# Reordering the heads and projections of a hybrid attention block on one Trainium2 core

## Time and profile before

| | |
|---|---|
| three runs | 743.0, 746.4, 747.96 us, median 746.4 |
| profiled execution, span from first to last instruction | 740.7 us |
| mean granted TensorE clock in it | 0.969 of full |
| PE busy | 695.3 us, 94% |
| DVE, ACT, POOL busy | 339.0, 278.3, 248.4 us |
| instructions | 9658 |

### The profile page before, as it was taken

How to read it: one execution, slowest core, us unless ns; L and a number is a source line. 1 busy time by engine, 2 the same in 40 slices (tenths; PEclk the granted TensorE clock), 3 DMA queues, 4 the chain that set the end, 5 groups by cost and what they waited for, 6 DMA issues and landing times.

```text
span 740.7 us, 9658 instructions
## 1 busy us (share of the span) xinstructions
PE 695.3 (94%) x3541; PEld 581.9 (79%) x3541; DVE 339.0 (46%) x819; ACT 278.3 (38%) x546; POOL 248.4 (34%) x121
## 2 busy tenths in 40 slices
PE   5998989999897997997999999999999999999995
PEld 4885678997797996786878888888888888888884
DVE  6521377577667778774436334334334321003004
ACT  4401565565454545552454323223223222114112
POOL 6601521031211211023317443544544434434422
PEclk7999999999999998999999999999999999999998
DMA  7447532031121111012315333323233233233202
GB/s 235 82 143 234 163 93 65 8 93 36 36 65 36 39 57 35 2 58 66 87 47 163 93 87 112 87 87 112 86 90 109 86 95 104 86 104 96 86 1 114
DMA packets 84227, 64.42 MB, mean 87 GB/s; under 512 B 2424, under 2 KB 75204, under 8 KB 84180
## 3 DMA queue, kind: packets, MB, share of 16 engines
q1 hardware_dynamic: 80160, 58.83, 26.9%
q10 hardware_dynamic: 3444, 4.48, 1.9%
q0 software_dynamic: 576, 0.49, 0.6%
HBM read 61.67 MB, written 4.47 MB: 89 GB/s over the span
## 4 chain that ended last, share of the span: by engine, by line
PE 84%; DVE 7%; DMA 4%; issue 3%; ACT 2%; SPq 0%; POOL 0%; DVEq 0%; ACTq 0%
PE bank L462 14%; PE bank L464 14%; PE bank L463 14%; PE bank L444 9%; PE bank L445 9%; PE bank L446 9%; PE bank L608 5%; DMA raw<-in_w_in_dram 4%; PE bank L585 3%; PE bank L569 2%; PE bank L570 2%; PE bank L456 2%; PE bank L519 1%; DVE bank L1054 1%; DVE k_diff L1035 1%
## 5 line engine op out<-in xcount | busy, mean ns | idle before, releaser
L420 POOL TENSOR_TENSOR w_lo<-raw,w_hi 128x1024 fp32r<-128x1024 f32 (+1 forms) x96 | 233.7, 2438 | 468.8 <-ACT w_hi L748 468.8
L748 ACT CAST w_hi<-raw 128x1024 fp32r<-128x1024 f32 (+1 forms) x96 | 100.4, 1050 | 275.3 <-PE bank L464 143.9
L462 PE MATMUL bank<-xT_hi,w_hi 128*128 128x512 f32 x480 | 191.9, 400 | 1.8 <-POOL w_lo L420 1.5
L464 PE MATMUL bank<-xT_hi,w_lo 128*128 128x512 f32 x480 | 190.0, 396 | 0.0
L463 PE MATMUL bank<-xT_lo,w_hi 128*128 128x512 f32 x480 | 189.6, 395 | 0.0
L462 PEld LDWEIGHTS bank<-xT_hi,w_hi 128*128 128x128 f32 x480 | 90.9, 189 | 21.7 <-POOL w_lo L420 2.0
L464 PEld LDWEIGHTS bank<-xT_hi,w_lo 128*128 128x128 f32 x480 | 91.0, 189 | 20.6
L463 PEld LDWEIGHTS bank<-xT_lo,w_hi 128*128 128x128 f32 x480 | 91.0, 190 | 18.2 <-issue 0.2
L816 ACT ACTIVATE E<-bank,nmax 128x128 f32<-128x128 f32 (+3 forms) x96 | 50.8, 529 | 76.3 <-DVE nmax L1054 76.2
L446 PE MATMUL bank<-w_hi,act_lo 128*128 128x512 f32 x176 | 69.0, 392 | 0.0
L444 PE MATMUL bank<-w_hi,act_hi 128*128 128x512 f32 x176 | 69.0, 392 | 0.0
(11 more groups left out here) (175 smaller groups left out, 934.2 us busy)
## 6 DMA issues: line engine op xcount, KB each, us to landing
raw<-in_w_gate_dram SPq DMA_DIRECT2D x22, 512.0 KB, 3.9
raw<-in_w_up_dram SPq DMA_DIRECT2D x22, 512.0 KB, 3.9
raw<-in_w_down_dram SPq DMA_DIRECT2D x22, 512.0 KB, 3.8
raw<-in_w_in_dram SPq DMA_DIRECT2D x20, 512.0 KB, 3.9
raw<-in_w_out_dram SPq DMA_DIRECT2D x8, 512.0 KB, 3.8
bias_rows<-bias_scratch ACTq DMA_DIRECT2D x1, 2304.0 KB
xres<-in_x_dram SPq DMA_DIRECT2D x4, 512.0 KB, 5.3
raw<-in_cmp_w_k_dram SPq DMA_DIRECT2D x4, 512.0 KB, 4.4
```

The source lines that it names most:

```text
L420: nc.gpsimd.tensor_tensor(wv_lo(k)[:, 0:n], raw[:, raw_of[("chunk", k)] % RAW_SLOTS, 0:n], wv_hi(k)[:, 0:n].bitcast(F32), ALU.subtract).th ...
L462: nc.tensor.matmul(bank[:, :], hi, xT_hi[:, kt, :], start=kt == 0, stop=False)
L464: return nc.tensor.matmul(bank[:, :], lo, xT_hi[:, kt, :], start=False, stop=kt == KT - 1)
L748: nc.scalar.copy(wv_hi(k)[:, 0:n], raw[:, raw_of[("chunk", k)] % RAW_SLOTS, 0:n]).then_inc(s_whi, 1)
```

## The change

- Order: `PROJ_JOBS` and `OUT_JOBS` name a fixed order of jobs. Compressed keys ("c") and their MLP ("h", "ht", "hc") move from the prologue into the loop, with w1 in four buffers of its own, which share memory with x; x is loaded a second time behind them. Slots: diff(1) comes ahead of nsa(2) and nsa(3).
- Filler: a planner gives each step its pieces by cost and by due steps, in place of a fixed rate. Evacuations are cut in units, which are laid on successive steps on ACT and DVE.
- Keys: for the differential heads the two maps keep their own halves and the second copy is made by four DMAs on POOL's queue (`double_keys`); for the NSA keys ACT writes hi twice and DVE subtracts twice.
- Bias rows are spread for each head by a DMA of SP, between weight loads.
- Roots: 1/sqrt is exp(-0.5 ln(.)), two activations on ACT, in place of Sqrt on ACT and small steps on DVE. In the head ACT takes all four squares. The last norm is made for each of the four tiles.
- w_out: the NSA part ("og") and the differential part ("od") are 4-piece jobs in the two projection banks. The transposes of `mix` are jobs ("mt").
- The last two chunks of w_down are done tile by tile (`last_rows`).
- Matmuls ahead of the head: 12 in place of 16, and 5, 3 and 5 between the row tiles.

```diff
-WARM = 16
+WARM = 12
+WARM_GAP = (5, 3, 5)
 RAW_SLOTS = 3
 SPLIT_SLOTS = 4
+W1_SLOTS = 4
 E_SLOTS = 4
 BIAS_SLOTS = 3
-PIECES = 8
-PIECES_PER_SLOT = 1.35
-LEAD_PIECES = 6
-FILL_RATE = 2.5
+LEAD_JOBS = 1
+AHEAD = {"q": 4, "k": 4, "dq": 4, "dk": 6, "dv": -2, "hc": 3}
...
+PROJ_JOBS = [("q", 0), ("k", "ksl"), ("vg", 0), ("vg", 1), ("k", "kw"),
+             ("q", 1), ("dq", 0), ("dk", 0), ("dv", (0, 0)), ("dv", (0, 1)), ("dq", 1), ("dk", 1), ("q", 2), ("c", 0),
+             ("c", 1), ("q", 3), ("h", 0), ("h", 1), ("dv", (1, 0)), ("ht", 0), ("dv", (1, 1)), ("hc", 0), ("dq", 2), ("dk", 2),
+             ("dk", 3), ("dq", 3)]
+OUT_JOBS = [("mt", 4), ("mt", 5), ("mt", 6), ("mt", 7), ("og", (0, 0)), ("og", (0, 1)), ("og", (0, 2)), ("og", (0, 3)), ("og", (1, 0)),
+            ("mt", 0), ("og", (1, 1)), ("mt", 1), ("og", (1, 2)), ("mt", 2), ("og", (1, 3)), ("mt", 3)]
+OUT_JOBS += [("od", (dh, t)) for dh in range(2) for t in range(NT)]
+BASE_JOBS = 4
+PIECES = {"ht": 1, "hc": 1, "mt": 1, "og": 4, "od": 4}
+PIECE_US = {"h": 0.86, "ht": 0.45, "hc": 0.9, "mt": 0.45, "dv": 0.73}
+ACT_UNITS = {"q": 2, "dq": 2, "k": 2, "dk": 2, "mt": 1}
+DVE_UNITS = {"q": 2, "dq": 2, "k": 2, "dk": 2, "c": 2}
...
-    nsa(0), nsa(1), diff(0), nsa(2), diff(1), nsa(3)
+    nsa(0), nsa(1), diff(0), diff(1), nsa(2), nsa(3)
...
+    own = [slot_us(x_) for x_ in slots] + [1.0] * 5
+    cost = [PIECE_US.get(jobs[j][0], 0.69) for j, _ in pieces]
+    due = [(s - ahead, 1 + max(n for n, (z, _) in enumerate(pieces) if z == j)) for s in range(n_slots)
+           for j, ahead in wanted(slots[s]) if j >= BASE_JOBS]
+    due.append((n_steps - 1, n_plan))
+    for s in range(n_steps):
+        rate = max((sum(cost[done:upto]) + sum(own[s:d + 1])) / (d + 1 - s) for d, upto in due if d >= s)
+        lag = min(lag + rate - own[s], 4.0)
+        must = max([upto for d, upto in due if d <= s] + [0])
+        while done < n_plan:
+            j, p = pieces[done]
+            if s < first_slot.get(jobs[j], 0) or (done >= must and lag < cost[done] / 2):
+                break
+            if p == 0 and any(ended[z] + ready(z) - (z == j - 2) > s for z in after(j)):
+                break
+            lag -= cost[done]
+            done += 1
+            ended[j] = s
+        piece_upto.append(done)
...
+            def load_w1(first, last):
+                for n in range(first, last):
+                    kv, p = n // 8, n % 8
+                    was = n - W1_SLOTS
+                    if was < 0:
+                        sp.wait_ge(s_norm, NT)
+                    elif was % 8 == 7:
+                        sp.wait_ge(s_job, job_of[("h", was // 8)] + 1)
+                    else:
+                        sp.wait_ge(s_w1, 7 * (was // 8) + was % 8 + 1)
+                    src = (cmp_w1_k, cmp_w1_v)[kv][0].rearrange("(j p) n -> p j n", p=P)[:, 2 * p:2 * p + 2, :]
+                    sp.dma_start(w1[:, n % W1_SLOTS, :].rearrange("p (k n) -> p k n", k=2), src).then_inc(s_w1raw[n % W1_SLOTS], 16)
...
+            def spread_bias(n):
+                h = bias_order[n]
+                if n >= 3:
+                    sp.wait_ge(s_spread[n % 3], 16 * (n // 3))
+                sp.dma_start(bias_rows[h, :, :], bias_scratch[h:h + 1, :].to_broadcast([P, 384])).then_inc(s_spread[n % 3], 16)
...
+                    sp.wait_ge(s_bvec, 1)
+                    sp.dma_start(bias_scratch[:, :], bias_vec[:, :]).then_inc(s_scratch, 16)
+                    sp.wait_ge(s_scratch, 16)
+                    for n in range(3):
+                        spread_bias(n)
...
+                if 8 <= k < 8 + NHEADS - 3:
+                    spread_bias(k - 5)
+                if chunks[k] == ("q", 3):
+                    load_w1(0, W1_SLOTS)
+                if chunks[k] == ("dk", 3):
+                    load_w1(W1_SLOTS, 16)
+                if chunks[k] == ("o", (0, 2)):
+                    sp.wait_ge(s_job, job_of[("h", 1)] + 1)
+                    for t in range(NT):
+                        sp.dma_start(xres[:, t, :], x[0, t * P:(t + 1) * P, :]).then_inc(s_x[t], 16)
...
+            def double_keys(j):
+                pool.wait_ge(s_evac, j + 1)
+                for hd in range(2):
+                    here, there = slice(hd * HD, (hd + 1) * HD), slice((1 - hd) * HD, (2 - hd) * HD)
+                    for z in range(2):
+                        k_ = k_diff[:, jobs[j][1] % 2, z, hd, :]
+                        pool.dma_start(k_[there, :], k_[here, :]).then_inc(s_dup[jobs[j][1]], 16)
+            for k in range(len(chunks)):
                 split(k)
-            for n, v in enumerate((lambda_q1, lambda_k1, lambda_q2, lambda_k2)):
-                pool.dma_start(lam_in[:, n, :], v[0].partition_broadcast(P)).then_inc(s_lamin, 16)
-            for n, v in enumerate((cmp_w2_k, cmp_w2_v)):
-                pool.dma_start(w2[:, n, :, :], v[0].rearrange("(m p) d -> p m d", p=P)).then_inc(s_small, 16)
-            pool.dma_start(cmask[:, :, :], c_cmask).then_inc(s_small, 16)
-            pool.dma_start(has_cmp[:, :], c_has).then_inc(s_small, 16)
-            for k in range(2, len(chunks)):
-                split(k)
+                if chunks[max(k - SPLIT_SLOTS, 0)][0] == "dk":
+                    double_keys(job_of[chunks[k - SPLIT_SLOTS]])
...
+            for t in range(NT):
+                pe.wait_ge(s_norm, t + 1)
+                turn_x(t, range(6))
+                if t == 1:
+                    pe.wait_ge(s_rows, 16 * 6)
+                    nc.tensor.transpose(ps[7][:, 0:N_ROWS], rows[0:N_ROWS, :], ident[0:N_ROWS, 0:N_ROWS]).then_inc(s_cols_t, 1)
+                if t < NT - 1:
+                    keep_warm(WARM_GAP[t])
...
+            for j, p in pieces[upto:]:
+                if jobs[j] == ("od", (1, 2)) and p == 0:
+                    pe.wait_ge(s_evac, job_of[("od", (0, 3))] + 1)
+                    for i in range(4):
+                        turn_residual(i)
+                proj_piece(j, p)
...
+            def last_rows(k, banks):
+                pe.wait_ge(s_split, k + 2)
+                for t in range(NT):
+                    for kw in (k, k + 1):
+                        for kk in range(2):
+                            f = 2 * chunks[kw][1][1] + kk
+                            hi, lo = wv_hi(kw)[:, kk * 512:(kk + 1) * 512], wv_lo(kw)[:, kk * 512:(kk + 1) * 512]
+                            mm = three(banks[t][:, :], act_hi[:, f, t * P:(t + 1) * P], act_lo[:, f, t * P:(t + 1) * P],
+                                       hi, lo, False, kw == k + 1 and kk == 1)
+                    mm.then_inc(s_last, 1)
...
+            def inverse_root(a, b, width, bias=None):
+                logs[0] += 1
+                nc.scalar.activation(stat[:, 32 + a:32 + b], stat[:, a:b], ACT.Ln, scale=1.0 / width,
+                                     bias=eps[:, 0:1] if bias is None else bias).then_inc(s_log, 1)
+                act.wait_ge(s_log, logs[0])
+                nc.scalar.activation(stat[:, 32 + a:32 + b], stat[:, 32 + a:32 + b], ACT.Exp, scale=-0.5).then_inc(s_root, 1)
...
+                elif kind == "dk":
+                    nc.scalar.activation(k_diff[half, a % 2, 0, unit, :], bank[half, :], ACT.Copy).then_inc(s_hi, 1)
+                else:
+                    k_ = k_nsa[:, 0, 2 * (a == "kw") + unit, :]
+                    nc.scalar.activation(k_[0:HD, :], bank[half, :], ACT.Copy).then_inc(s_hi, 1)
+                    nc.scalar.activation(k_[HD:P, :], bank[half, :], ACT.Copy).then_inc(s_hi, 1)
...
+                if s == n_slots + 4:
+                    act.wait_ge(s_sums, 16)
+                    inverse_root(12, 16, P)
                 if 3 <= s < n_slots + 3:
                     copy_turned(s - 3)
+                for j, u in act_units[s]:
+                    evac_hi(j, u)
...
+                if s - 6 in cmp_slot:
+                    t = cmp_slot.index(s - 6)
+                    act.wait_ge(s_of, turn[s - 6] + 1)
+                    square(mix[:, t, 512:1024], mixT_lo[:, t % 2, :], 16 + t, 4 + t)
+                    if t == NT - 1:
+                        act.wait_ge(s_ss, 8)
+                        inverse_root(16, 20, 512)
+                for h, a, b in ((1, 0, 8), (2, 8, 12)):
+                    if s == last_diff_qk[h] + 6:
+                        act.wait_ge(s_sums, b)
+                        inverse_root(a, b, P)
...
+                elif kind == "dk":
+                    dve.wait_ge(s_hi, hi_before[j] + unit + 1)
+                    hi, lo = (k_diff[half, a % 2, z, unit, :] for z in range(2))
+                    ins = nc.vector.tensor_tensor(lo, bank[half, :], hi.bitcast(F32), ALU.subtract)
                 else:
-                    for hd in range(2):
-                        src = bank[hd * HD:(hd + 1) * HD, :]
-                        dve.wait_ge(s_hi, hi_upto[k] - 1 + hd)
-                        if kind in ("q", "dq"):
-                            q = q_nsa[:, 2 * a + hd, :] if kind == "q" else q_diff[:, a % 2, hd, :]
```

(24 more changed lines are left out.)

979 lines of the change are left out of this document (451 added, 528 removed).

## The result

Predicted were 724 us, between 703 and 741. Measured were **749.2 us** (median, 747.8 to 753.8) against 744.6 us for the kernel before in the same runs: ratio 1.0049, 95% interval 1.0025 to 1.0073. The gain that I had expected is not there, and the time lies outside my range. It lies inside the range of rival C (734 to 754), "the gain is eaten".

What follows compares the result with a forecast made beforehand. PE's stream of work was taken as the bound, with 44 us of holes and low clock to win. Span 740.7 - 44 + 3 (head) + 3 (tail) + 16 (staying) = 718.7, plus 5.7 to the median: 724 us, range 703 to 741.

Steps and rivals of the forecast that it cites:

- rival C: Loop: PE's holes move rather than go, the late part runs at DVE's pace; 734 to 754 us, chance 0.18.
- What stays in the loop: Loop ahead of the feed-forward part: of 44 us of PE holes and low clock, 16 us stay.
- Late part: Steps 77 to 93, little filler: DVE cannot keep ahead, 10 us stay.
- my bound from above: Late part at worst: the 11.3 us lost there in the kernel before and 5 more.
- today's row: Stage 284 to 334 us of the kernel before: 6.3 us idle PE plus 5.0 us lower clock, 11.3 us.
- Held DVE steps: Loop: DVE steps on one column, held under a POOL split, still cost 2 us.
- End of the differential part: Scaling of the last differential head, 3.3 us of filler over a chain of about 4: of 5.7 us 2 stay.
- Keys doubled by DMA: Differential keys in the loop: POOL's DMAs cost nothing, and the waits behind the key copies go.
- Tail: After the last matmul: ACT's roots with two table loads per tile fall behind PE; 11.2 us against 8.4, +2.8 us.
- Head: Before the first projection matmul: four roots with table loads of 1.28 us; start near 23 us against 21.39, +3 us.
- Rival B: Head, tail and loop: Ln and Exp share one table set, no extra loads; 708 us (703 to 714), chance 0.16.
- SyncE's order: SP's load of chunk 3 behind its wait for the bias vector: PE needs it 11 us later, so nothing.

Runs made afterwards that it cites:

- root_late: Kernel after with POOL's splits in quarters, plus the NSA norm's squares and root four steps later on ACT: 740.3 us, against 740.6 without the later root.
- after_evac_first: Kernel after with VectorE's evacuations ahead of bias addition and weighing in steps 87 to 93: 751.5 us, ratio to before 1.0086.
- root_late_evac_first: root_late with VectorE's evacuations ahead of bias addition and weighing in steps 87 to 93: 736.8 us, ratio to before 0.9867.
- one_set_split4: Kernel after with one table set for Ln and Exp loaded and POOL's splits in quarters: 729.4 us, ratio to before 0.9793.

## Why the prediction was wrong, step by step

**The step that failed: "What stays in the loop", 16 us.** Measured are 39.4: 23.4 of the 27.3 us by which the span (746.0) passed my 718.7. Its parts:

- *Late part, 10 us, and 2 more for the root at step 89.* 24.2 us, beyond even my bound from above (11.3 and 5 more). I saw that the steps there hold 0 to 3 pieces, and then priced it as VectorE's busy time ("DVE cannot keep ahead"), near today's row. VectorE is busy 36.6 of 54 us. What costs is latency: with no filler between them, transposes, hi part, lo part and the next transposes form one chain over three engines, and what stands in a queue ahead of its link delays the chain, unless another queue holds it longer. I had the root at 2 us of its own; the root and VectorE's order hold the same wait, and the experiments show that taking away one of them gives no time and both 3.8 us (root_late, after_evac_first, root_late_evac_first). Clock was in the row I went by, 5.0 of its 11.3 us; measured are 7.0. So the miss is idle PE time: 17.2 us, where that row has 6.3.
- *Held DVE steps, 2 us.* Too small: quarters brought 8.6 us. I had seen how a split holds VectorE and put it down to the copies, so that it would go with them. It holds other steps as well, at 318.36 a one-column product for 2.37 us, and early in the loop the gates (below). The two stages ahead of 276 us lose 13.1 us together, and these 2 were all that the sum had for them.
- *End of the differential part, 2 us:* 2.1 us, in waits of 1.1 us or less.

The hole at 60 us, of which the sum had nothing:

```profile
55.77 2.40 POOL L507 TENSOR_TENSOR w_lo<-raw,w_hi 128x1024 fp32r<-128x1024 f32 x1 [1.24 <-ACT w_hi L833]
55.97 2.27 DVE L1267 TENSOR_SCALAR gates<-gates 128x96 f32<-128x96 f32 x1
...
61.44 0.58 ACT L909 ACTIVATE E<-bank,nmax 128x384 f32<-128x384 f32 x1 [3.91 <-DVE nmax L1162]
61.71 1.40 DVE L1140 TENSOR_TENSOR k_nsa<-bank,k_nsa 64x512 fp32r<-64x512 f32 x2
```

The two extra subtractions for the NSA keys, costed at nothing "in steps with room", follow a held step, and PE waits 3.6 us for them; with quarters it is 2.1.

The Trainium skill (SBUF — State Buffer, "SBUF: two separate sides") states that VectorE and GpSimd share a port pair as an exclusive lock for a whole instruction, VectorE steps with two inputs in SBUF among them when the GpSimd instruction reads SBUF. The trace agrees: 2.37 us for one column under a whole split, 0.73 under a quarter.

**Keys doubled by DMA, nothing on the cost side, the gain within the 44:** right. There is no wait for the doubled keys in the list, and the part alone is worth 11.5 us on the kernel before; inside the new order undoing it costs 6.3 to 8.

**Tail, +2.8 us:** +5.7. The seven loads and the two in each root were right; missed was that the next tile's addition stands behind the wait for the root, 3.6 us in three gaps. The output after the last root came 0.7 us shorter than I had it.

**Head, +3 us:** +1.8. The seven loads more were right, and so was the price of 1.28 us for a change of function: the last root ends at 19.8 us where I had 19.5. The 1.3 us added behind it for casts and fewer warm matmuls did not come. Rival B, one set for both functions, is not what the kernel did. The Trainium skill (ScalarE: Activation LUTs, "Table sets: the hidden batching unit") has one load for ln then exp; here every Ln and every Exp had its own until the set was loaded by hand, and then the rule held, with 5 loads. It was worth 11.6 us where B said 16: the wait for chunk 3 that it uncovered, and more time at half clock in its profiled execution, stand on the other side.

**SyncE's order, nothing:** no wait for chunk 3 stands in the kernel after's list, so right, but with no margin. At a head 8.5 us shorter it costs 6.

**Rival C** had the size (22 us or more in the late part; 734 to 754) and a chance of 0.18, but half its mechanism: there was no pace of VectorE, and the loss of 98 to 276 (7.6 us) was as C said, half of before. (Its chances don't quite agree: half of it within 1% of 746 in one place, two thirds in the sum.)

What remains of the difference in span, 2.3 us, is PE's work by this measure: 309.4 us between the first projection and 372, against 306.6, less 0.5 us in the feed-forward part. No run tells whether it is work or short waits that the records put into busy time. The 5.7 us that I added from span to median are not "start and end of an execution": in the executions listed since, the time is 1.8 to 2.1 us above the span (747.9 against 746.0 for the one profiled here), so the rest was that the profiled execution before was a quick one.

## What to carry to other kernels

Where filler runs out, a stage is priced by the latency of its chain, with what stands ahead of each link in every queue, and not by busy shares; with VectorE busy 68% it lost 24 us. A remedy that gives nothing alone is no proof against a cause: look whether a second cause holds the same wait, and take both away once. Before a change of order is judged, take its parts one by one: one part gave 11.5 us here and the others took back 15. And compare executions by idle time before length: two of one program differed by 4.7 us in the loop through the clock.

## What the hardware showed beyond that

Quartering a POOL subtraction of 128x1024 costs POOL time (8 quarters 6.08 us, two whole ones 4.67) and still won about 8 us on each of three kernels, since what a long one holds is another engine. A wait on PE can cost more than itself: in one_set_split4 the 3.8 us wait for chunk 3 was worth 6.0 us when removed, with the stretch at 1.2 GHz from 29 to 36 us gone with it.
